# Attention stage of a two-block transformer kernel: constant matrices and the stick-breaking operand in one-pass mode, the operand split into a high and a low part

## The reference, cut to what matters

```
def stick_breaking_attention(q, k, v):          # 4 heads of 64
    z = einsum('bqhd,bkhd->bhqk', qb, k) * scale
    mask = kpos[None, :] < qpos[:, None]
    log_1m = where(mask, log_sigmoid(-z), 0.0)
    rest = cumsum(log_1m, axis=3, reverse=True) - log_1m
    wts = where(mask, exp(log_sigmoid(z) + rest), 0.0)
    return einsum('bhqk,bkhd->bqhd', wts, v)

def mla_attention(q_nope, q_rope, k_nope, k_rope, v):   # latent attention, 4 heads
    s = (q_nope . k_nope + q_rope . k_rope) * scale
    s = where(kpos <= qpos, s, -inf)
    return softmax(s) @ v
```

## Time and profile before

| | us |
|---|---|
| median of 3 runs | 4018.66 (4003.91 to 4023.31) |
| the profiled execution, own time | 4018.41 |
| its span, first to last instruction | 4016.6 |
| PE busy in the span | 3822.4 (95%) |
| DVE / ACT busy | 2086.2 (52%) / 1313.2 (33%) |
| attention stage, layer 0 | 2199.7 to 2304.6 |
| attention stage, layer 1 | 3426.4 to about 3531.8 |

### The profile page before, as it was taken

The page is one execution under the profiler, slowest core; times in us unless marked ns, Lnnn a source line. Parts: engine busy times, 40 slices in busy tenths (PEclk is TensorE's granted clock), DMA queues, the critical chain, the costliest instruction groups (busy, mean ns, idle before and its releaser), DMA issues.

```text
span 4016.6 us, 70955 instructions
## 1 busy us (share of the span) xinstructions
PE 3822.4 (95%) x30798; PEld 3148.8 (78%) x30798; DVE 2086.2 (52%) x2910; ACT 1313.2 (33%) x1901; POOL 145.6 (4%) x195
## 2 busy tenths in 40 slices
PE   7998968989999999999989999999999988999998
PEld 5766768887868888888877688887888878688887
DVE  4967466755454445334755453344333755553335
ACT  4244333313333223222423532223222342532222
POOL 0000012220000000000000000000000000000000
PEclk9999979999999999999999999999999999999999
DMA  6213000024342233333102033332333202023331
GB/s 253 70 54 115 11 3 3 3 73 142 126 142 95 95 104 95 103 97 105 59 3 88 3 118 95 95 100 90 105 95 105 70 13 68 22 93 102 95 105 53
DMA packets 317735, 327.81 MB, mean 82 GB/s; under 512 B 8016, under 2 KB 241504, under 8 KB 316016
## 3 DMA queue, kind: packets, MB, share of 16 engines
q1 hardware_dynamic: 310064, 286.87, 22.3%
q0 software_dynamic: 7360, 36.40, 2.5%
HBM read 314.86 MB, written 8.39 MB: 80 GB/s over the span
## 4 chain that ended last, share of the span: by engine, by line
PE 83%; DVE 9%; ACT 4%; issue 2%; DMA 1%; POOL 0%; DVEq 0%; ACTq 0%; SPq 0%
PE psum L247 82%; DVE arena L301 2%; PE psum L254 2%; ACT arena L351 1%; DVE ring L301 1%; DVE arena L312 1%; DVE ring L332 1%; DVE r L301 1%; ACT ring L351 1%; ACT r L351 1%; DMA ring<-in_w_ada 1%; DVE arena L332 0%; DVE arena L316 0%; DMA ring<-in_w_in 0%; DVE ring L308 0%
## 5 line engine op out<-in xcount | busy, mean ns | idle before, releaser
L247 PE MATMUL psum<-r 128*128 128x512 f32 (+2 forms) x12960 | 2854.0, 381 | 31.3 <-DVE r L301 29.3
L247 PEld LDWEIGHTS psum<-r 128*128 128x128 f32 x12960 | 2343.0, 188 | 509.2 <-DVE r L301 30.9
L301 DVE TENSOR_TENSOR r<-ring,r 128x2048 fp32r<-128x2048 f32 (+1 forms) x259 | 573.2, 2213 | 308.7 <-ACT r L351 305.1
L351 ACT ACTIVATE r<-ring 128x2048 fp32r<-128x2048 f32 (+1 forms) x259 | 478.2, 1846 | 366.4 <-PE psum L247 309.7
L351 ACT ACTIVATE arena<-psum 128x512 f32<-128x512 f32 (+6 forms) x505 | 266.0, 527 | 976.4 <-PE psum L247 903.5
L301 DVE TENSOR_TENSOR arena<-arena,psum 128x512 f32<-128x512 f32 (+4 forms) x209 | 130.9, 626 | 571.5 <-PE psum L247 553.9
L247 PE MATMUL psum<-arena 64*64 64x64 f32 (+10 forms) x5262 | 391.2, 261 | 27.4 <-DVE arena L316 9.2
L247 PEld LDWEIGHTS psum<-arena 64*64 64x64 f32 (+4 forms) x5262 | 271.6, 152 | 125.9 <-issue 62.6
L247 PE MATMUL psum<-ring 64*64 64x64 f32 (+3 forms) x7792 | 296.9, 231 | 43.7 <-ACT ring L351 17.0
L247 PEld LDWEIGHTS psum<-ring 64*64 64x64 f32 (+2 forms) x7792 | 256.7, 141 | 65.1 <-issue 28.9
L351 ACT ACTIVATE r<-arena 128x512 fp32r<-128x512 f32 (+2 forms) x188 | 113.1, 602 | 503.7 <-DVE arena L301 500.8
(11 more groups left out here) (123 smaller groups left out, 1610.1 us busy)
## 6 DMA issues: line engine op xcount, KB each, us to landing
ring<-in_ffa_w_in SPq DMA_DIRECT2D x88, 512.0 KB, 4.8
ring<-in_ffb_w_in SPq DMA_DIRECT2D x88, 512.0 KB, 4.6
ring<-in_w_mlp SPq DMA_DIRECT2D x32, 1024.0 KB, 5.2
ring<-in_w_in SPq DMA_DIRECT2D x31, 1024.0 KB, 5.2
ring<-in_w_ada SPq DMA_DIRECT2D x24, 1024.0 KB, 5.2
ring<-in_mix_w_in SPq DMA_DIRECT2D x24, 1024.0 KB, 5.1
ring<-in_ffa_w_out SPq DMA_DIRECT2D x20, 1024.0 KB, 4.9
ring<-in_ffb_w_out SPq DMA_DIRECT2D x20, 1024.0 KB, 4.9
```

The lines of the kernel that those rows point to most:

```text
L247: ins = self.raw.matmul(o, l, r, start=start, stop=stop, skip_group_check=True)
L301: self.done(self.raw and self.raw.tensor_tensor(o, a, b, f), keys)
L351: self.done(self.raw and self.raw.activation(o, i, f, scale=scale, bias=bias), keys)
```

## The change

The stick-breaking softplus is split into a high part `SPhi` (fp32r, by ACT) and a low part `SPlo` (fp32r, by DVE, in place of SP), in a new turn p that follows m. The turns a and b multiply the triangle and the ones with both parts in fp32r. The constants come from the fp32r table, which ACT rounds once, in front of layer 0's `act_sb_in`. The masks of both attentions use it too. PE waits for `sb sp lo` in place of `sb sp`. The turn p0 stands between m0 and h0, p1 between m1 and b0, p2 and p3 after r4 and r9, each in front of its a.

```
+    m.SPlo = [view(K.rounded(mk_h + 2048 * z, 2048), [512, 4], [1, 512]) for z in range(2)]
+    first = [K.rounded(SLOT * NSLOT + 6144 + 512 * z, 512) for z in range(2)]
+    m.SPhi = [[first[z]] + [m.SPlo[z][:, 4 - s, 0:512 - 128 * s] for s in (1, 2, 3)] for z in range(2)]

+def act_tables(E, K):
+    a = ScalarLine(E, "sb")
+    a.wait_ge(*K.at("in", "consts again"))
+    for name in ("nUI128", "nLI128", "negLT", "negGE"):
+        a.copy(K.R[name], K.C[name], ("sb tables",))

-ATTENTION_TURNS = ("z0 e0 v0 z1 e1 v2 l0 m0 h0 l1 h1 h2 h3 a0 r0 m1 b0 r1 o0 z2 r2 e2 r3 l2 m2 r4 a1 r5 b1 r6 o1 z3 r7 e3 r8 l3 m3 r9 "
-         "a2 r10 b2 r11 o2 r12 a3 s0 r13 b3 r14 s1 r15 o3 r16 s2 r17 T s3 t").split()
+ATTENTION_TURNS = ("z0 e0 v0 z1 e1 v2 l0 m0 p0 h0 l1 h1 h2 h3 a0 r0 m1 p1 b0 r1 o0 z2 r2 e2 r3 l2 m2 r4 p2 a1 r5 b1 r6 o1 z3 r7 e3 "
+         "r8 l3 m3 r9 p3 a2 r10 b2 r11 o2 r12 a3 s0 r13 b3 r14 s1 r15 o3 r16 s2 r17 T s3 t").split()

 def pe_sb(E, K, l, kind, h):
+    t.wait_ge(*K.at("sb tables"))
+    SP, WT = [m.SPhi[h % 2], [m.SPlo[h % 2][:, s, 128 * s:512] for s in range(4)]], m.eb[h % 2]
     elif kind in "ab":
-        t.wait_ge(*K.at("sb sp", l, h))
+        t.wait_ge(*K.at("sb sp lo", l, h))
...
             t.mm(o[:, 0:N], k[:, lo:lo + 128], q[:, lo:512], True, False)
-            t.mm(o[:, 0:N], C["nLI128"], SP[:, s, lo:512], False, False)
+            for x in SP:
+                t.mm(o[:, 0:N], R["nLI128"], x[s], False, False)
             for j in range(s + 1, 4):
                 c = 128 * (j - s)
-                t.mm(o[:, c:N], C["none"], SP[:, j, 128 * j:512], False, False)
-            t.mm(o[:, 0:128], C["ident"], C["negGE"], False, True, ("sb w", l, h, s))
+                for x in SP:
+                    t.mm(o[:, c:N], R["none"], x[j], False, False)
+            t.mm(o[:, 0:128], R["ident"], R["negGE"], False, True, ("sb w", l, h, s))

 def act_sb(E, K, l, kind, h):
+    elif kind == "p":
+        for s in range(4):
+            a.wait_ge(*K.at("sb sp", l, h, s))
+            a.copy(m.SPhi[h % 2][s], m.SP[h % 2][:, s, 128 * s:512], ("sb sp hi", l, h, s))

 def dve_sb(E, K, l, kind, h):
-            v.tt(SP[:, s, lo:lo + 128], SP[:, s, lo:lo + 128], K.C["US128"], MUL, ("sb sp", l, h))
+            v.tt(SP[:, s, lo:lo + 128], SP[:, s, lo:lo + 128], K.C["US128"], MUL, ("sb sp", l, h, s))
+    elif kind == "p":
+        for s in range(4):
+            v.wait_ge(*K.at("sb sp hi", l, h, s))
+            v.tt(m.SPlo[h % 2][:, s, lo:512], SP[:, s, lo:512], m.SPhi[h % 2][s], SUB, ("sb sp lo", l, h))

 def pe_mla(E, K, l, kind, n):
-            t.mm(o[:, N - 128:N], C["ident"], C["negLT"], False, True, ("mla s", l, n))
+            t.mm(o[:, N - 128:N], R["ident"], R["negLT"], False, True, ("mla s", l, n))
```

More of the change, by code:

```diff
@@ L976, in memory @@
     m.pT = [view(lend(512), [128, 4], [1, 128]) for _ in range(2)]
+    m.SPlo = [view(K.rounded(mk_h + 2048 * z, 2048), [512, 4], [1, 512]) for z in range(2)]
+    first = [K.rounded(SLOT * NSLOT + 6144 + 512 * z, 512) for z in range(2)]
+    lend(1024)
+    m.SPhi = [[first[z]] + [m.SPlo[z][:, 4 - s, 0:512 - 128 * s] for s in (1, 2, 3)] for z in range(2)]
     m.sq, m.st = m.tmp[:, 0:512], m.tmp[:, 512:640]
@@ L3644, in dve_sb_in @@
     E.ahead()
-ATTENTION_TURNS = ("z0 e0 v0 z1 e1 v2 l0 m0 h0 l1 h1 h2 h3 a0 r0 m1 b0 r1 o0 z2 r2 e2 r3 l2 m2 r4 a1 r5 b1 r6 o1 z3 r7 e3 r8 l3 m3 r9 "
-         "a2 r10 b2 r11 o2 r12 a3 s0 r13 b3 r14 s1 r15 o3 r16 s2 r17 T s3 t").split()
+ATTENTION_TURNS = ("z0 e0 v0 z1 e1 v2 l0 m0 p0 h0 l1 h1 h2 h3 a0 r0 m1 p1 b0 r1 o0 z2 r2 e2 r3 l2 m2 r4 p2 a1 r5 b1 r6 o1 z3 r7 e3 "
+         "r8 l3 m3 r9 p3 a2 r10 b2 r11 o2 r12 a3 s0 r13 b3 r14 s1 r15 o3 r16 s2 r17 T s3 t").split()
 def take_turns(sb, mla):
     for turn in ATTENTION_TURNS:
-        (sb if turn[0] in "zelmabosT" else mla)(turn[0], int(turn[1:] or 0))
+        (sb if turn[0] in "zelmpabosT" else mla)(turn[0], int(turn[1:] or 0))
 def pe_sb(E, K, l, kind, h):
-    t, m, C = TensorLine(E, "sb"), K.m, K.C
+    t, m, R = TensorLine(E, "sb"), K.m, K.R
     if kind == "T":
@@ L3668, in pe_sb @@
     q, k = m.sqkT[hp, h // 2, :], m.sqkT[hp, 2 + h // 2, :]
-    SP, WT = m.SP[h % 2], m.eb[h % 2]
+    t.wait_ge(*K.at("sb tables"))
+    SP, WT = [m.SPhi[h % 2], [m.SPlo[h % 2][:, s, 128 * s:512] for s in range(4)]], m.eb[h % 2]
     if kind == "z":
@@ L3740, in dve_sb @@
             v.tt(SP[:, s, lo:512], SP[:, s, lo:512], e[:, s, lo:512], ADD)
-            v.tt(SP[:, s, lo:lo + 128], SP[:, s, lo:lo + 128], K.C["US128"], MUL, ("sb sp", l, h))
+            v.tt(SP[:, s, lo:lo + 128], SP[:, s, lo:lo + 128], K.C["US128"], MUL, ("sb sp", l, h, s))
+    elif kind == "p":
+        for s in range(4):
+            lo = 128 * s
+            v.wait_ge(*K.at("sb sp hi", l, h, s))
+            v.tt(m.SPlo[h % 2][:, s, lo:512], SP[:, s, lo:512], m.SPhi[h % 2][s], SUB, ("sb sp lo", l, h))
     elif kind == "o":
@@ L3776, in pe_mla @@
 def pe_mla(E, K, l, kind, n):
-    t, m, C = TensorLine(E, "mla"), K.m, K.C
+    t, m, R = TensorLine(E, "mla"), K.m, K.R
     ukv = view(m.ukv[:, 0, 0:], [1, 512])
@@ L4087, in scalar_program @@
         E.meet(f"delta rule done {l}")
+        if l == 0:
+            act_tables(E, K)
         act_sb_in(E, K, l)
```

## The result

| | before | after |
|---|---|---|
| median | 4019.57 us (4003.91 to 4023.31, 4 runs) | 4063.52 us (4051.97 to 4068.66, 4 runs) |
| ratio to before | | 1.0106, interval 1.0086 to 1.0126 |
| profiled execution, own time / span | 4018.41 / 4016.6 us | 4051.97 / 4050.1 us |
| attention stage, layer 0 / layer 1 | 104.93 / 109.29 us | 123.83 / 123.76 us |
| the rest of the span | 3802.4 us | 3802.5 us |

The forecast was 4024.4 us in 4003 to 4038, "no change". The changed kernel is slower by 1.1%, some 43 us, and each stage is 124 us long where the prediction gave 102 to 110. A stage is counted here, in all kernels alike, from the start of its first score product to the first product of the output projection (in layer 1 that is 4 us later than the end used in the earlier trace rows).

The account below looks back on a forecast made before the run. It took DVE and ACT to bound head 0 and PE heads 1 to 3. Span 4016.6 + 1.4 (chain less savings) + 4.6 (clock) = 4022.6, plus 1.8 outside the span, gave 4024.4 us, range 4003 to 4038.

Parts of the forecast that it names:

- What PE saves when it runs at the upper level: Turns a and b: faster triangle and ones products save PE 1.8 us a head, 14.6 in all.
- The chain of head 0: Head 0: p0 and p1 delay ACT and DVE, a0 about 2 us later, o0 5.7; plus 5.1 a layer.
- That the clock would fall near o0: At o0 and z2: the granted clock drops to 0.5 after the new pause.
- the 6.4 us pause ahead of o0: Ahead of o0: PE has almost nothing to do for some 6.4 us while ACT finishes b0's late exps.
- the clock's term: At o0 and z2: lower clock costs 2.3 us a layer, 4.6 in all, with ends 0 and 9.4.
- the forecast's two terms: Both layers: plus 1.4 us (head 0's delay less the gain of heads 1 to 3) and 4.6 for the clock.
- the mask in r ... I take 0: Masks in fp32r, 16 a layer: between 0 and 0.11 us saved each, taken as 0; other end 3.5 in all.
- one of 128 from 0.24 to 2 x 0.11, which is nearly nothing: Triangle and ones, 128 columns: two fp32r products of 0.11 us replace one of 0.24, almost no gain.
- what the sum had for them: Heads 1 to 3: faster products shorten each layer by 4.4 us, bounds 0 and 5.4.
- Rival 2: Ahead of o0: the pause keeps the clock low through b1, 9.1 us a layer, time 4037; chance 0.12.
- Rivals 1 and 3: Attention: PE bounds and the split is hidden, 4003.8, chance 0.17; or the products get no faster, 4057, chance 0.03.

Follow-up runs that it names:

- c3: After with tile 3 unsplit and in f32 and the masks in f32, the wider products still split in fp32r; 1.0016, 4019.02 us.
- c1: After with triangle, ones and masks all in f32, while the p turns, their copies, subtractions and waits stay; 1.0032, 4029.73 us.
- b2: After without the p turns: SP written once in fp32r and multiplied twice, so exponents are wrong; 1.0035, 4036.33 us.
- b1: After with triangle and ones multiplying unsplit SP in f32; p turns, waits and fp32r masks stay; 1.0056, 4034.80 us.
- d3: After with masks in f32 and six of a head's eight tile 3 fp32r products streamed 256 columns wide; 1.0033, 4025.40 us.
- e1: After with head 0 unsplit in f32, head 1's split moved later, masks in f32, six of eight tile 3 products 256 wide; 1.0018, 4019.34 us.
- d2: After with tile 3 unsplit and in f32, the masks staying in fp32r; 1.0043, 4027.03 us.
- c2: After with head 1 in f32 and without p1, head 0 still split; 1.0058, 4039.99 us.
- d4: After with twenty unread fp32r products of 512 columns added ahead of a1 in each layer; 1.0111, 4054.55 us.
- b4: After with head 0 unsplit in f32, head 1's copies moved behind b0 and its subtractions behind r3; 1.0076, 4046.96 us.
- c4: After with head 0 unsplit in f32, head 1's split moved later, tile 3 unsplit in f32 and masks in f32; 0.9977, 4005.65 us.

## Why the prediction was wrong

*Point by point.* What PE saves when it runs at the upper level was right: tile 0 of a3 takes 2.57 us for the 2.59 of the sum (1.57 and the first product's 1.02), tile 1 takes 1.81 for 2.46 before, 0.65 saved where 0.51 was counted. The chain of head 0 was right: from the start of the stage a0 is 2.7 us later (predicted 2.1: the four subtractions took 2.28), m1 starts at 2229.47 (2229.3), b0's exps at 2233.49 (2233.3), and o0 is 5.9 + 0.3 = 6.2 us later counted from the start of the stage (5.7). ACT is the releaser before o0, and in the two profiled executions nothing outside the stages moved. That the clock would fall near o0 was right but late: it fell at a0 already, behind p0's pause, which the prediction counted as 2.1 us of delay and not as a place for a fall. With that the 6.4 us pause ahead of o0, on which the clock's term rested, did not come about: 1.27 us of it were left.

*The step that failed* is the clock's term in the sum: 2.3 us a layer, ends 0 and 4.7. It took the length of the fall from the earlier trace rows, where it passes within a1, and let it end with z2. It lasted 75 us in each layer. What that costs is read from c3, which has both pauses, p0's 0.4 us shorter: 28.6 us of both stages for 106 us more at the lower level, and 36 us by the ratios. That is 14 to 18 us a layer where the term had 2.3. Without the long stay the sum agrees: c3 came out at 1.0016, 6.4 us above before (1.6 to 11.2), and the forecast's two terms together were 6.0; the interval is wide for a sum of that size.

*Behind it stood a second one*: "the mask in r ... I take 0", "one of 128 from 0.24 to 2 x 0.11, which is nearly nothing". These products were priced by their own time alone. Their price was in what the clock did around them: leaving both kinds in f32 takes 0.90% away. The wide products save about what the sum had for them, 8.8 us (4.4 a layer): from c1 to c3, where they are the difference, the ratio falls by 0.16%, 6 us, and the median by 10.7; the intervals of the two ratios overlap, so the size is not better known. The pauses alone (c1) cost 13 us, for 10.2 in the sum (5.1 a layer) and what the clock adds.

*The rivals.* Rival 2 had the mechanism and the point from which it decides, "about 10 us", but let the lower level end after b1 and so came to 4037. Rivals 1 and 3 fell: the releasers at a0 and o0 are those of the forecast, and the products did get faster. The quoted section of the Trainium skill ("TensorE: Matmul & The Clock Gate", "HAM oscillation — how this bites in real kernels") agrees with most falls: they follow a wait at a0, at r2 to r4 and, in the run b2, at r0, of 1.40 to 2.85 us. It is no rule here, since in b1 the clock stayed full behind the 2.85 us at a0. The section "What's actually happening" on that page of the Trainium skill adds that activity releases the throttle. Here the trace speaks against that as a rule for what the profile calls busy: 46.00 of 46.00 us busy at 0.50 in after.

*What stays open.* Shown is that narrow fp32r products add time at the lower level, each kind by itself, in both orders of the turns. Not shown is by what property. Doubling the width of six in eight changed nothing that the runs can tell (d3, e1), which speaks against width, but the masks and the last two weren't widened. The number and time of the records are the same for tile 3 in both modes (d2), which speaks against them and for the mode; for the masks an f32 product differs from an fp32r one in mode, records and duration at once. The shorter p of the kernels with tile 3 in f32 was not tried by itself. Nor is it known what ends a stretch: in c2 and in layer 0 of d4 it ended after 27 us, ahead of a1, among products that are those of after. The 57 us between the ten executions of b4 go with the clock (0.971 and 0.956 in the fastest and the slowest); why the clock differs from one execution to the next is part of the same question.

## What to carry to other kernels

Before products are moved to a faster mode in a stage that has waits, look at the granted clock row by row: a pause costs not only itself but slows every product behind it until the clock is back, and how long that takes can change with the change. Compare several executions, since one and the same program had stretches of 27 and of 75 us. Move the wide products and leave the narrow ones, whose own gain is nothing, as they are; put the preparation of the new operand behind the work that releases PE. Here that turned 1.0106 into 0.9977.

## What the runs showed of the hardware

- A stretch at the lower level lasted 75 us in both stages of after (72 us in b4, 89 in b2), 46 of them with PE busy in the profile without a gap. In c1, c3 and c4, without narrow fp32r products but with waits of up to 3.2 us, stretches lasted 3 to 14 us.
- A microsecond at the lower level cost about 0.27 us of the stage by the profiles of after and c3 (28.6 us for 106). Between executions of one kernel it mostly cost more: in b4 the fastest (4015.11 us, clock 0.971) and the slowest (4072.19, 0.956) differ by 57 us for some 125 us at the lower level, 0.46; a straight line through the ten executions gives 0.42 there and 0.27 to 0.43 in the other kernels of ten runs. All stay under the 0.5 of work that only PE bounds at half rate; that the rest is waits for ACT and DVE which the slower PE fills is an explanation that fits o0 in after (1.27 us of wait where b1, with the clock full until then, has 3.81), and was not tested.
- The spread of a kernel's executions is a spread of the clock: before had 0.38 to 0.41 us more for each microsecond at the lower level in its runs on the three chips.
- fp32r and f32 products slow down alike: the nine fp32r records of tile 0 take 2.75 us from first start to next form at the lower level (2253.90 to 2256.65) and 1.52 at the upper (2306.40 to 2307.92), the f32 product of 512 columns 2.00 and 1.05.
